# The v rows of the context's experts, one token at a time, on TensorE's column groups

## The chip, the cores and the metric
One core of one Trainium2 chip runs the whole program. The metric is the device time of one execution in microseconds. All data is f32.

## The reference
Two blocks of two layers each, on 256 tokens of width 1024. The first block is dense, the second has a feed-forward of experts (PEER): every token picks 8 x 16 of 16384 experts, and each expert is one row of a table `u` and one row of a table `v`.

```python
def first_block(x, ...):
    for l in range(2):
        h = rmsnorm(x, norm_mix[l])
        ... = split(h @ w_in[l])
        mix = concatenate([mlstm(...), moba(...), nsa(...)])
        x = x + mix @ w_out[l]
        u = square(relu(rmsnorm(x, norm_ffn[l]) @ w_ff1[l]))
        x = x + u @ w_ff2[l]
    return x

def peer_block(hb, w_q, sub_keys, u_tab, v_tab):
    ...
    expert = take_along_axis(cand_i, pos, axis=-1)
    g = softmax(top_s)
    u = u_tab[expert]
    act = gelu(einsum('nhkd,nd->nhk', u, hb))
    w = g * act
    return einsum('nhk,nhkd->nd', w, v_tab[expert])

def second_block(x, c, ctx, c_ctx, ...):
    xc = ctx
    for i in range(2):
        h, hc = modulate(rms_norm(x)), modulate(rms_norm(xc))
        x = x + g1 * (attention(q, concatenate([kc, k]), concatenate([vc, v])) @ w_o[i])
        if i == 0:
            xc = xc + cg1 * (context_attention(qc, kc, vc) @ w_o[i])
        x = x + g2 * peer_ffn(modulate(rms_norm(x)), ...)
        if i == 0:
            xc = xc + cg2 * peer_ffn(modulate(rms_norm(xc)), ...)
    return x
```

The change is about the last line, the experts of the 256 context tokens in layer 0 of the second block. They depend on nothing of the first block.

## The kernel before
**Stages.** The program has six in a row: `attention(part="context")` from 0 to some 323 us; `first_blocks`, layer 0 to 849 us and layer 1 from 885 to 1404; `attention(part="latents")` to 1708; `experts` of the latents; `attention(part="last")`; `experts` of the last layer to the end. Each engine has its own function in a stage (`sync`, `scalar`, `vector`, `gpsimd`, `tensor`), and runs it in the order in which it is written, with semaphore waits between the engines. There is no planner: the order is written by hand.

**PSUM.** `Stage` (L101) deals out the eight banks as four pairs in rotation, by a list of groups. `freed(g)` is the wait of PE for a pair, `empties(g)` its release.

**The experts of the context** are the class `Beside` (L1195), done beside `first_blocks` and the latents' attention. 256 tokens are two tiles of 128 partitions, and a tile has 128 rows of each table: row n is, for each of the 128 tokens, its n-th expert. So one row is one gather of 128 x 1024 f32, 0.52 MB, an indirect DMA that POOL issues (L1266). There are four slots for u rows and four for v rows. A step s of `vector` (L1219) is a dot of u row s with the normed tokens (L1237), and an accumulation of v row s - 16 times its weight into the context's residual `xc` (L1256). After every eight dots come some small operations of DVE (L1227 to L1246) and one power on POOL (L1278) for the gelu. `gpsimd` (L1268) issues the gathers and waits until the step that used a slot before is done.

**Where the steps stand.** `beside.vector(e, n)` is written into the vector function of each stage: 47 steps in layer 0's mixing, of them 25 in its attention part, 56 in its feed-forward, 101 in layer 1 in the same places, the remaining 68 through the latents' attention (`more(n)`, L480). `mark` notes how many steps are placed where DVE hands POOL a variance, so that POOL's gathers up to there stand ahead of its power (L1930, L744).

**A layer of the first block** (`tensor`, L1945): the turned activations hT; the projections (q and k, gates, o and v as L174 matmuls); M, the mLSTM's gates spread by a selector (L1993); the remaining projections `nat` 1 and 2; the head turns QT; the compression cmp; scores, softmax and outputs of six pairs of heads, in ping-pong with DVE and ACT (the attention part); the turn of the mix (mixT); `wo`; ff1 in eight chunks, ff2 in eight chunks (L2159). At the end of layer 0's ff2 DVE does the routing of heads 4 to 7 of the second tile of context tokens (`routed`, L1897), through ACT's exponentials `head_exp` (L1600).

**The latents' attention** (`attention`, L181): hT, three projections of q, k and v, then DVE norms and rotates queries and keys (L602) ahead of five turns QT, then 16 heads, a softmax each.

**The modulation** (L763) is in the context stage: weights of 128 x 2, 512 columns, outputs at partitions 0, 32, 64 and 96.

## Time and profile before

| what | value |
|---|---|
| median of 3 runs | 3325.4 us (3320.01 to 3327.51) |
| span of the profiled execution | 3318.4 us |
| PE busy | 2516.6 us, 76% |
| DVE busy | 2160.5 us, 65% |
| POOL busy | 1324.5 us, 40% |
| ACT busy | 475.9 us, 14% |
| moved by DMA | 1046.73 MB, mean 315 GB/s |
| of it by the gathers' queue (q0) | 805.37 MB |

The span is the time from the first to the last instruction of one execution; the runs are timed separately and contain a little more. Busy times are sums over the whole program and say which engine has work, not which one is waited for.

### The profile page before, as it was taken

The numbers are of one execution on the slowest core, as the hardware profiler recorded it, in microseconds if no ns is written. First come the engines' busy times: TensorE is split into PE (matmuls) and PEld (weight loads), VectorE is DVE, ScalarE is ACT, GpSimd is POOL, SyncE is SP. The second block draws the span as 40 slices with busy tenths as digits, with TensorE's granted clock in tenths as the row PEclk, the third lists the DMA queues.
The fourth block names the chain that finished last, engine by engine and source line by source line (L and its number), as shares of the span: only waits on it lengthen the run. The fifth ranks groups of instructions, "written<-read, shape, count | busy, mean of one in ns | idle before, by whom it ended". The sixth has DMA issues, their size and how long they took to land. (4 is left out here: it accounts for less than half of the span.)

```text
span 3318.4 us, 25154 instructions
## 1 busy us (share of the span) xinstructions
PE 2516.6 (76%) x7884; PEld 1405.9 (42%) x7884; DVE 2160.5 (65%) x5153; ACT 475.9 (14%) x1396; POOL 1324.5 (40%) x1096
## 2 busy tenths in 40 slices
PE   6785883899586599951667888887767688888877
PEld 2354553684344376421443334343334434434332
DVE  1438458678777856648867776777436577767774
ACT  1210111000111100000111111111112111111111
POOL 0000216444553755535735444454300144444542
PEclk9998885999787699975788999999978889899998
DMA  6656748889785899996849999999751399999996
GB/s 261 256 216 232 262 148 270 304 333 351 270 337 190 276 335 384 347 338 226 283 161 419 418 418 418 422 421 421 324 188 51 117 419 419 419 419 421 421 421 280
DMA packets 249209, 1046.73 MB, mean 315 GB/s; under 512 B 20550, under 2 KB 53430, under 8 KB 176884
## 3 DMA queue, kind: packets, MB, share of 16 engines
q0 software_dynamic: 147456, 805.37, 61.5%
q1 hardware_dynamic: 93456, 222.23, 18.1%
q10 hardware_dynamic: 8164, 17.53, 1.5%
q8 instruction: 63, 1.03, 0.1%
q14 instruction: 70, 0.57, 0.1%
HBM read 1041.28 MB, written 3.77 MB: 315 GB/s over the span
## 5 line engine op out<-in xcount | busy, mean ns | idle before, releaser
L1266 POOL DMA_INDIRECT sb_beside_slots<-in_peer_uv,sb_beside_chosen x512 | 596.2, 1164 | 433.5 <-DVE sb_xc L1256 284.6
L1237 DVE SCALAR_TENSOR_TENSOR sb_beside_slots<-sb_beside_slots,sb_beside_H 128x1024 f32<-128x1024 f32 x256 | 313.1, 1224 | 221.9 <-DMA sb_beside_slots<-in_peer_uv,sb_beside_chosen 214.9
L1256 DVE SCALAR_TENSOR_TENSOR sb_xc<-sb_beside_slots,sb_beside_small,sb_xc 128x1024 f32<-128x1024 f32 x254 | 325.8, 1283 | 4.6 <-DMA sb_beside_slots<-in_peer_uv,sb_beside_chosen 1.8
L174 PE MATMUL psum<-sb_f_arena,sb_f_ring 128*128 128x256 f32 (+1 forms) x1344 | 295.9, 383 | 7.9 <-issue 7.9
L174 PEld LDWEIGHTS psum<-sb_f_arena,sb_f_ring 128*128 128x128 f32 (+1 forms) x1344 | 251.5, 188 | 51.8 <-issue 9.9
L174 PE MATMUL psum<-sb_f_ring,sb_f_arena 128*128 128x512 f32 (+2 forms) x448 | 196.5, 601 | 5.7 <-DVE sb_f_arena L1877 5.7
L1170 PE MATMUL psum<-sb_latents_ring,sb_latents_scores 128*128 128x512 f32 x304 | 149.1, 643 | 52.3 <-ACT sb_latents_scores L1128 52.3
L1170 PE MATMUL psum<-sb_last_ring,sb_last_scores 128*128 128x512 f32 x276 | 141.7, 665 | 52.9 <-ACT sb_last_scores L1128 37.9
L1170 PE MATMUL psum<-sb_beside_slots,sb_latents_scores 128*128 128x512 f32 x288 | 139.8, 631 | 34.6 <-ACT sb_latents_scores L1128 34.6
L2159 PE MATMUL psum<-sb_f_ring,sb_f_arena 128*128 128x512 f32 x384 | 165.4, 592 | 0.0
L1026 POOL DMA_INDIRECT sb_latents_ring<-in_peer_uv,sb_latents_scores x76 | 92.7, 1220 | 130.6 <-PE psum L1170 92.5
L174 PEld LDWEIGHTS psum<-sb_f_ring,sb_f_arena 128*128 128x128 f32 x448 | 87.7, 197 | 109.9 <-issue 103.6
L1026 POOL DMA_INDIRECT sb_last_ring<-in_peer_uv,sb_last_scores x69 | 78.7, 1141 | 137.3 <-PE psum L1170 99.2
L1060 DVE SCALAR_TENSOR_TENSOR sb_latents_ring<-sb_latents_ring,sb_latents_H 128x1024 f32<-128x1024 f32 x76 | 92.0, 1223 | 49.4 <-DMA sb_latents_ring<-in_peer_uv,sb_latents_scores 49.4
L1026 POOL DMA_INDIRECT sb_beside_slots<-in_peer_uv,sb_latents_scores x72 | 86.8, 1205 | 88.3 <-PE psum L1170 80.0
L1060 DVE SCALAR_TENSOR_TENSOR sb_beside_slots<-sb_beside_slots,sb_latents_H 128x1024 f32<-128x1024 f32 x72 | 87.5, 1223 | 48.2 <-DMA sb_beside_slots<-in_peer_uv,sb_latents_scores 48.2
L1170 PEld LDWEIGHTS psum<-sb_latents_ring,sb_latents_scores 128*128 128x128 f32 x304 | 61.4, 207 | 133.7 <-issue 71.8
L1060 DVE SCALAR_TENSOR_TENSOR sb_last_ring<-sb_last_ring,sb_last_H 128x1024 f32<-128x1024 f32 x69 | 83.6, 1223 | 47.3 <-DMA sb_last_ring<-in_peer_uv,sb_last_scores 47.3
L1170 PEld LDWEIGHTS psum<-sb_last_ring,sb_last_scores 128*128 128x128 f32 x276 | 57.6, 213 | 130.4 <-issue 84.1
L2159 PEld LDWEIGHTS psum<-sb_f_ring,sb_f_arena 128*128 128x128 f32 x384 | 72.9, 190 | 91.4 <-issue 91.4
L1170 PEld LDWEIGHTS psum<-sb_beside_slots,sb_latents_scores 128*128 128x128 f32 x288 | 56.4, 200 | 110.9 <-issue 65.5
L744 POOL TENSOR_TENSOR sb_last_small<-sb_last_small,sb_consts 128x8 f32<-128x8 f32 (+2 forms) x6 | 7.9, 1324 | 225.0 <-DVE sb_last_small L164 154.1
(543 smaller groups left out, 4771.9 us busy)
## 6 DMA issues: line engine op xcount, KB each, us to landing
sb_f_ring<-in_w_ff SPq DMA_DIRECT2D x32, 2048.0 KB
sb_context_ring<-in_ada_w SPq DMA_DIRECT2D x23, 2048.0 KB, 10.7
sb_f_ring<-in_w_in SPq DMA_DIRECT2D x8, 2048.0 KB
sb_f_ring<-in_w_in SPq DMA_DIRECT2D x6, 1904.0 KB
sb_context_ring<-in_peer_w_q SPq DMA_DIRECT2D x8, 1024.0 KB, 10.0
sb_beside_slots<-in_peer_uv,sb_beside_chosen POOLq DMA_INDIRECT x512
sb_f_ring<-in_w_out SPq DMA_DIRECT2D x4, 2048.0 KB
sb_latents_ring<-in_peer_w_q SPq DMA_DIRECT2D x8, 1024.0 KB, 18.2
```

Source lines behind the costliest of these rows:

```text
L174: last = e.matmul(out, a, b, start=(i == 0), stop=(i == len(terms) - 1))
L744: e.tensor_tensor(r[:, 0:n], r[:, 0:n], C("m05")[:, 0:n], ALU.pow).then_inc(rstd, 1)
L1026: e.indirect_dma_start(out=slots[n % ns], out_offset=None, in_=table, in_offset=bass.IndirectOffsetOnAxis(ap=rt["idx"][:, q % 4, k:k + 1], ...
L1060: e.scalar_tensor_tensor(out=u_of(n), in0=u_of(n), scalar=1.0, in1=H[:, turns[n // TOPK][0], :], op0=ALU.mult, op1=ALU.mult, accum_out=rt[ ...
L1170: done = e.matmul(st.pair(("acc", g))[:, half, :], diag[:, n % (4 * BATCH), :], v_of(n)[:, half * 512:(half + 1) * 512], start=(f == 0 and ...
L1237: e.scalar_tensor_tensor(out=self.u_slot[s % 4], in0=self.u_slot[s % 4], scalar=1.0, in1=self.H[:, s // (PH * TOPK), :], op0=ALU.mult, op1 ...
L1256: e.scalar_tensor_tensor(out=acc, in0=row, scalar=wn, in1=acc, op0=ALU.mult, op1=ALU.add).then_inc(self.added, 1)
L1266: return e.indirect_dma_start(out=to, out_offset=None, in_=self.table, in_offset=bass.IndirectOffsetOnAxis(ap=at, axis=0), element_offset= ...
L2159: done = e.matmul(acc[t][:, half, :], u_part[c][:, f * S + t * P:f * S + (t + 1) * P], w[:, f, half * 512:(half + 1) * 512], start=False, ...
```

## The change
The u dots stay as they are on DVE. The v rows change their shape: one gather now fetches the 128 experts of *one token* onto 128 partitions, and PE sums them over the partitions with the token's 128 weights as the stationary operand.

- The indices and the weights of a tile are turned by PE (`turn_idx`, `turn_weights`), after a cast on DVE, and kept in SBUF (`keep_idx`, `keep_weights`). The gelu of a tile is done once for all 128 rows: `low` and `weigh` on DVE, a tanh on ACT. POOL's powers for it are gone.
- `columns` is a field of 4 x 16 weight matrices of 128 x 32, zero but for one column each. It lies in the space of `xc`. POOL clears it and copies 64 tokens' weights to its diagonal, twice a tile (`set_columns`).
- Four tokens are a group: 8 matmuls (L1339) with 32 weight columns and 512 moving columns, for tokens 32 partitions apart, into the last pair of PSUM. A tile has 32 groups that accumulate there. So the stages `first_blocks` and latents have three pairs for everything else. ACT copies the sums out (`tile_summed`, `all_summed`), and the latents' experts wait for it (`summed`, 3).
- One ring of eight slots serves u and v rows. The order is u rows 0 to 143, v rows of tile 0, u rows 144 to 255, v rows of tile 1.
- Where they stand: 65 dots in layer 0's mixing (25 in its attention part), 79 in its feed-forward, none in layer 1's mixing, 100 in its feed-forward (10 to each chunk of ff1, 20 after), 12 at the start of the latents' attention. The 32 groups of tile 0 stand in layer 1's mixing on PE: 2 ahead of hT, 6 after v, 4 ahead of `nat` 1, 4 after `nat` 2, 4 after the first two QT, 4 after the first turned softmax, 4 after the turned compressed keys, 4 after the fifth scores. Those of tile 1 in the latents' attention: 2 after hT, 2 after each projection and 4 more, 1 after each of five QT, 1 after each of 15 heads.
- `block.tensor` is written ahead of `block.gpsimd` in `Stage.run`, since POOL's marks now need PE's places too.

```diff
@@ class Stage
-    def __init__(self, nc, sems, psum, order, after=None):
+    def __init__(self, nc, sems, psum, order, after=None, pairs=4):
@@ class Beside
-    LAG, DEEP = 16, 4
-    STEPS = 2 * PH * TOPK + 16
+    SLOTS, GROUPS, AHEAD = 8, 32, 8
+    STEPS = NT * PH * TOPK
+    EARLY = 144
...
+    def tensor(self, e, groups):
+        upto = min(self.at_tensor + groups, NT * self.GROUPS)
+        for n in range(self.at_tensor, upto):
+            t, i = divmod(n, self.GROUPS)
+            if i % 16 == 0:
+                e.wait_ge(self.columns_set, n // 16 + 1)
+            rows = [self.landed_row(e, ("v", 4 * n + j)) for j in range(4)]
+            for half in range(2):
+                for j in range(4):
+                    done = e.matmul(self.sums[32 * j:32 * j + 32, half, :], self.columns[:, j, i % 16, :], rows[j][:, half * 512:(half + 1) * 512], start=(i == 0), stop=(i == self.GROUPS - 1))
+            done.then_inc(self.added, 1)
+        self.at_tensor = upto
...
+    def set_columns(self, e, a):
+        t, half = divmod(a, 2)
...
+        e.wait_ge(self.wT_ready, t + 1)
+        if a == 0:
+            e.memset(self.columns[:, :, :, :], 0.0).then_inc(self.cleared, 1)
...
+        e.tensor_copy(diagonal(half), weights).then_inc(self.columns_set, 1)
+
+    def gather(self, e, i):
+        kind, n = self.rows[i]
+        if i >= self.SLOTS:
+            was, m = self.rows[i - self.SLOTS]
+            e.wait_ge(*((self.dotted, m + 1) if was == "u" else (self.added, m // 4 + 1)))
...
@@ first_block, tensor
+        rows(2)
...
             natural(name, weights_of(name), 0, MW)
+        rows(6)
         sel = C("sel").rearrange("p (h m) -> p h m", h=4)
         ps = claim("M")
...
+        rows(4)
         e.wait_ge(*landed(("nat", 1)))
         natural(("nat", 1), weights_of(("nat", 1)), 0, 476)
+        mark(1)
...
         natural(("nat", 2), weights_of(("nat", 2)), 0, 476)
+        rows(4)
...
         heads_turned(1)
+        rows(4)
...
         p_turned(0)
+        rows(4)
@@ attention, tensor
-        for c, g in qkv:
+        rows(2)
+        for n, (c, g) in enumerate(qkv):
             e.wait_ge(*landed(wqkv_of[c]))
             project(("qkv", c, g), weights_of(wqkv_of[c]), (g, g + 1))
+            mark(n + 1)
+            rows(2)
+        rows(4)
@@ first_block, vector
-            beside.vector(e, 2 if routes else 4)
+            beside.vector(e, 10 if last else 6 if routes else 8)
```

PE where layer 1 begins, from ff2 of layer 0 to the remaining projections. Before (L168 is the turn hT, L174 the projections, L1993 is M):

```order
L168 MATMUL psum<-sb_consts,sb_f_hn 128x128 x16
L174 MATMUL psum<-sb_f_arena,sb_f_ring 128x256 x64
L174 MATMUL psum<-sb_f_arena,sb_f_ring 4x256 x16
L174 MATMUL psum<-sb_f_ring,sb_f_arena 128x468 x16
L174 MATMUL psum<-sb_f_ring,sb_f_arena 128x512 x32
L1993 MATMUL psum<-sb_f_hn,sb_consts 128x256 x4
L168 MATMUL psum<-sb_consts,sb_f_hn 128x4 x4
L174 MATMUL psum<-sb_f_ring,sb_f_arena 128x476 x16
L2008 MATMUL psum<-sb_f_attn 128x256 x4
L2012 MATMUL psum<-sb_f_attn 128x128 x4
```

Now (L1339 are the groups, eight matmuls each; L2132 is M):

```order
L1339 MATMUL psum<-sb_beside_slots,sb_xc 32x512 x16
L168 MATMUL psum<-sb_consts,sb_f_hn 128x128 x16
L174 MATMUL psum<-sb_f_arena,sb_f_ring 128x256 x64
L174 MATMUL psum<-sb_f_arena,sb_f_ring 4x256 x16
L174 MATMUL psum<-sb_f_ring,sb_f_arena 128x468 x16
L174 MATMUL psum<-sb_f_ring,sb_f_arena 128x512 x32
L1339 MATMUL psum<-sb_beside_slots,sb_xc 32x512 x48
L2132 MATMUL psum<-sb_f_hn,sb_consts 128x256 x4
L168 MATMUL psum<-sb_consts,sb_f_hn 128x4 x4
L1339 MATMUL psum<-sb_beside_slots,sb_xc 32x512 x32
L174 MATMUL psum<-sb_f_ring,sb_f_arena 128x476 x16
L2149 MATMUL psum<-sb_f_attn 128x256 x4
```

Two groups stand ahead of the turn hT, six between the projections and M, four between the gates' turn and the next projection.

PE in layer 1's attention part now, from the turn of the first softmax (L2191 are scores, L2231 is the compressed keys' projection):

```order
L168 MATMUL psum<-sb_consts,sb_f_attn 128x128 x4
L1339 MATMUL psum<-sb_beside_slots,sb_xc 32x512 x32
L168 MATMUL psum<-sb_consts,sb_f_arena 128x128 x12
L2231 MATMUL psum<-sb_f_cw,sb_f_small 15x64 x2
L168 MATMUL psum<-sb_consts,sb_f_attn 128x128 x8
L174 MATMUL psum<-sb_f_N,sb_f_attn 128x64 x4
L2191 MATMUL psum<-sb_f_arena 128x128 x4
L174 MATMUL psum<-sb_f_N,sb_f_attn 128x64 x8
L2191 MATMUL psum<-sb_f_arena 128x256 x4
L168 MATMUL psum<-sb_consts,sb_f_kv 128x15
L1339 MATMUL psum<-sb_beside_slots,sb_xc 32x512 x32
L168 MATMUL psum<-sb_consts,sb_f_attn 128x128 x4
```

Four groups stand behind the first turned softmax, and four more behind the turned compressed keys (`sb_f_kv`); before, these places had nothing between their neighbours.

POOL from the last rows of layer 0 to the first of layer 1. Before (L1924 and L1926 are the norm of layer 1's input, L1278 the gelu's power):

```order
L1266 DMA sb_beside_slots<-in_peer_uv,sb_beside_chosen 128x1024 x7
L1924 TENSOR_SCALAR sb_f_small<-sb_f_small 128x1
L1926 TENSOR_TENSOR sb_f_small<-sb_f_small,sb_consts 128x1
L1924 TENSOR_SCALAR sb_f_small<-sb_f_small 128x1
L1926 TENSOR_TENSOR sb_f_small<-sb_f_small,sb_consts 128x1
L1266 DMA sb_beside_slots<-in_peer_uv,sb_beside_chosen 128x1024 x9
L1278 TENSOR_TENSOR sb_beside_small<-sb_consts,sb_beside_small 128x8
L1266 DMA sb_beside_slots<-in_peer_uv,sb_beside_chosen 128x1024 x16
L1278 TENSOR_TENSOR sb_beside_small<-sb_consts,sb_beside_small 128x8
```

Now (L2053 and L2055 are that norm, L2059 the powers of the mixing; `sb_beside_small` holds the turned indices, so its gathers are v rows):

```order
L1382 DMA sb_beside_slots<-in_peer_uv,sb_beside_chosen 128x1024 x71
L1382 DMA sb_beside_slots<-in_peer_uv,sb_beside_small 128x1024 x4
L2053 TENSOR_SCALAR sb_f_small<-sb_f_small 128x1
L2055 TENSOR_TENSOR sb_f_small<-sb_f_small,sb_consts 128x1
L2053 TENSOR_SCALAR sb_f_small<-sb_f_small 128x1
L2055 TENSOR_TENSOR sb_f_small<-sb_f_small,sb_consts 128x1
L1382 DMA sb_beside_slots<-in_peer_uv,sb_beside_small 128x1024 x4
L1358 MEMSET sb_xc 128x2048
L1364 COPY sb_xc<-sb_beside_chosen 128x4x16
L1382 DMA sb_beside_slots<-in_peer_uv,sb_beside_small 128x1024 x48
L2059 TENSOR_TENSOR sb_f_small<-sb_f_small,sb_consts 128x2x8
L1382 DMA sb_beside_slots<-in_peer_uv,sb_beside_small 128x1024 x16
```

The last u rows and the first four v rows stand ahead of the norm; behind it come four v rows, then the columns' clearing and copy, then 48 v rows (12 groups) ahead of the first power of the mixing.

## Rows read from the trace of the kernel before

**Rows 1.** page, part 1 and the slices: busy us of PE, and GB/s
```profile
PE 2516.6 (76%) x7884; PEld 1405.9 (42%) x7884; DVE 2160.5 (65%) x5153; ACT 475.9 (14%) x1396; POOL 1324.5 (40%) x1096
...
GB/s 261 256 216 232 262 148 270 304 333 351 270 337 190 276 335 384 347 338 226 283 161 419 418 418 418 422 421 421 324 188 51 117 419 419 419 419 421 421 421 280
```

**Rows 2.** busy time by stretch: PE, PEld, DVE, ACT, POOL, clock, DMA share, GB/s
```profile
440.00:584.00 144.00, 75.86 (x381) 63.06 (x379) 113.50 (x230) 23.68 (x69) 75.27 (x58) 0.64 0.66 223
892.00:1000.00 108.00, 97.78 (x311) 57.97 (x310) 77.27 (x138) 15.00 (x26) 58.52 (x47) 0.91 0.84 315
1000.00:1139.00 139.00, 73.08 (x366) 60.82 (x365) 113.00 (x230) 22.72 (x68) 74.28 (x58) 0.63 0.68 230
1180.00:1292.00 112.00, 111.72 (x515) 97.96 (x516) 74.78 (x113) 8.11 (x8) 64.20 (x54) 1.00 0.98 372
1500.00:1560.00 60.00, 8.52 (x28) 6.38 (x28) 48.00 (x83) 2.99 (x5) 35.35 (x26) 0.50 0.60 202
```

**Rows 3.** page, part 5: the groups of the rows beside
```profile
L1266 POOL DMA_INDIRECT sb_beside_slots<-in_peer_uv,sb_beside_chosen x512 | 596.2, 1164 | 433.5 <-DVE sb_xc L1256 284.6
L1237 DVE SCALAR_TENSOR_TENSOR sb_beside_slots<-sb_beside_slots,sb_beside_H 128x1024 f32<-128x1024 f32 x256 | 313.1, 1224 | 221.9 <-DMA sb_beside_slots<-in_peer_uv,sb_beside_chosen 214.9
L1256 DVE SCALAR_TENSOR_TENSOR sb_xc<-sb_beside_slots,sb_beside_small,sb_xc 128x1024 f32<-128x1024 f32 x254 | 325.8, 1283 | 4.6 <-DMA sb_beside_slots<-in_peer_uv,sb_beside_chosen 1.8
```

**Rows 4.** groups by line, DVE, from 466 to 584 (layer 0's attention part)
```profile
L1256 DVE SCALAR_TENSOR_TENSOR sb_xc<-sb_beside_slots,sb_beside_small,sb_xc 128x1024 f32<-128x1024 f32 x24 | 30.7, 1281 | 0.1
L1237 DVE SCALAR_TENSOR_TENSOR sb_beside_slots<-sb_beside_slots,sb_beside_H 128x1024 f32<-128x1024 f32 x25 | 30.4, 1218 | 11.4 <-DMA sb_beside_slots<-in_peer_uv,sb_beside_chosen 11.3
```

**Rows 5.** groups by line, DVE, from 1446 to 1708 (latents' front)
```profile
L1256 DVE SCALAR_TENSOR_TENSOR sb_xc<-sb_beside_slots,sb_beside_small,sb_xc 128x1024 f32<-128x1024 f32 x63 | 80.7, 1281 | 3.3 <-DMA sb_beside_slots<-in_peer_uv,sb_beside_chosen 1.8 <-DMA sb_latents_mod<-kept_mod 0.5
L1237 DVE SCALAR_TENSOR_TENSOR sb_beside_slots<-sb_beside_slots,sb_beside_H 128x1024 f32<-128x1024 f32 x49 | 59.9, 1221 | 43.1 <-DMA sb_beside_slots<-in_peer_uv,sb_beside_chosen 42.9
```

**Rows 6.** waits of PE, 330 to 1720: total, times, longest
```profile
PE psum L168 <- DVE sb_latents_scores L602: 60.3, 3, 32.0
...
PE psum L168 <- DVE sb_f_small L1854: 21.3, 2, 10.6
PE psum L174 <- DVE sb_f_kv L1812: 18.9, 2, 9.4
```

**Rows 7.** timeline of PE, layer 1's mixing: start, us, idle before
```profile
884.84 3.91 PE L168 MATMUL psum<-sb_consts,sb_f_hn 128*128 128x128 f32 x16 [35.81 <-ACT sb_f_hn L1502]
...
978.22 3.75 PE L1993 MATMUL psum<-sb_f_hn,sb_consts 4*128 4x256 f32 x8 [10.22 <-DVE sb_f_hn L1655]
...
1000.37 12.94 PE L174 MATMUL psum<-sb_f_ring,sb_f_arena 128*128 128x476 f32 x32
...
1132.66 3.67 PE L168 MATMUL psum<-sb_consts,sb_f_hn 128*128 128x128 f32 x16 [14.85 <-DVE sb_f_hn L1792]
1139.49 30.24 PE L174 MATMUL psum<-sb_f_ring,sb_f_arena 128*128 128x512 f32 x64 [3.16 <-DVE sb_f_arena L1877]
```

**Rows 8.** timeline of PE: two bursts of the modulation, one of ff2
```profile
103.40 3.51 PE L763 MATMUL psum<-sb_context_ring,sb_cvec 128*2 128x512 f32 x16 [4.51 <-DMA sb_context_ring<-in_ada_w]
108.37 1.90 PE L763 MATMUL psum<-sb_context_ring,sb_cvec 128*2 128x512 f32 x16 [1.46 <-DMA sb_context_ring<-in_ada_w]
...
738.12 41.36 PE L2159 MATMUL psum<-sb_f_ring,sb_f_arena 128*128 128x512 f32 x96
```

**Rows 9.** timeline of POOL and DVE from 490 to 496: gathers, and a dot
```profile
490.92 1.01 POOL L1266 DMA_INDIRECT sb_beside_slots<-in_peer_uv,sb_beside_chosen  x1 [0.19 <-issue]
...
492.24 0.94 POOL L1266 DMA_INDIRECT sb_beside_slots<-in_peer_uv,sb_beside_chosen  x1 [0.30 <-issue]
...
495.38 1.23 DVE L1237 SCALAR_TENSOR_TENSOR sb_beside_slots<-sb_beside_slots,sb_beside_H 128x1024 f32<-128x1024 f32 x1 [0.96 <-DMA sb_beside_slots<-in_peer_uv,sb_beside_chosen]
```

**Rows 10.** weight loads: modulation (20 to 120), and projections (page, part 5)
```profile
L763 PEld LDWEIGHTS psum<-sb_context_ring,sb_cvec 128*2 128x2 f32 x128 | 3.1, 95 | 35.6 <-DMA sb_context_ring<-in_ada_w 22.4 <-issue 13.3
...
L174 PEld LDWEIGHTS psum<-sb_f_arena,sb_f_ring 128*128 128x128 f32 (+1 forms) x1344 | 251.5, 188 | 51.8 <-issue 9.9
```

More of the change, by code:

```diff
@@ L482, in more @@
                 beside.vector(e, steps)
+        n_marks = [0]
         def mark():
             if beside:
-                beside.mark((part, sum(1 for m in beside.marks if m[0] == part)))
+                beside.mark_vector((part, n_marks[0]))
+                n_marks[0] += 1
+        more(Beside.STEPS)
+        if beside:
+            beside.low(e, 1)
         e.wait_ge(*st.computed("cT"))
@@ L741, in gpsimd @@
             if beside:
-                beside.gpsimd(e, beside.marks[part, turn] + 1)
+                beside.gpsimd(e, beside.marks[part, turn])
             e.wait_ge(var, turn + 1)
@@ L812, in tail_group, with rows, mark @@
                 transposes(group, rows2)
+        def rows(n):
+            if beside:
+                beside.tensor(e, n)
+        def mark(turn):
+            if beside:
+                beside.mark_tensor((part, turn))
+        if beside:
+            beside.turn_weights(e, 1)
+        mark(0)
         if context:
@@ new lines, in gpsimd @@
+    def gpsimd(self, e, done):
+        dots, weights, groups = done
+        over = next((i for i, (kind, n) in enumerate(self.rows) if n >= (dots if kind == "u" else 4 * groups)), len(self.rows))
+        while self.at_gpsimd < len(self.actions):
+            what, i = self.actions[self.at_gpsimd]
+            if i >= over + self.AHEAD if what == "gather" else (i // 2 >= weights or 16 * i > groups):
+                break
+            (self.gather if what == "gather" else self.set_columns)(e, i)
+            self.at_gpsimd += 1
@@ L1621, in vector, with dots @@
         own = Tally(dve)
+        def dots(n):
+            if not gone:
+                beside.vector(e, n)
         if gone:
             e.wait_ge(gone.squared, 8)
+        else:
+            beside.cast_idx(e, 0)
         e.memset(QKp[:, :, 0:3], 0.0).then_inc(*own.up())
@@ L1634, in vector @@
                     e.scalar_tensor_tensor(out=qk[:, b, :], in0=QKp[:, b, j:j + S], scalar=cols[:, b, j:j + 1], in1=qk[:, b, :], op0=ALU.mult, op1=ALU.add).then_inc(*own.up())
-            beside.vector(e, 3)
+            dots(4)
+            if not gone and i == 0:
+                beside.keep_idx(e, 0)
         e.wait_ge(*own.now)
@@ L1828, in vector @@
         heads_out(1)
-        beside.vector(e, 2)
+        dots(2)
         scores(3)
@@ L1842, in vector @@
         dens(2)
-        beside.vector(e, 2)
+        dots(2)
         scores(4)
-        beside.vector(e, 1)
+        dots(1)
         e.wait_ge(p_exp, 1)
@@ L1855, in vector @@
         dens(3)
-        beside.vector(e, 2)
+        dots(2)
         e.wait_ge(*st.computed("cy"))
@@ L2120, in tensor @@
         scores(5)
+        rows(Beside.GROUPS - beside.at_tensor if gone else 0)
         p_turned(4)
@@ L2146, in tensor @@
             done.then_inc(st.mm, 1)
+            if last and c == 3:
+                beside.turn_idx(e, 1)
         acc = [claim(name) for name in accs]
@@ L2156, in tensor @@
                 blocks[l + 1].column_group(e)
+            if c == 6 and not last:
+                beside.turn_weights(e, 0)
             for f, t in [(f, t) for f in range(4) for t in range(NT)] if c < 7 else [(f, t) for t in range(NT) for f in range(4)]:
```

311 lines of the change are left out of this document (187 added, 124 removed).

## Prediction

> **What bounds the kernel now.** I read the page first. The line of PE shows 2516.6 us of 3318.4 busy, and the line of GB/s shows a plateau of 418 to 422 GB/s in the slices of both expert stages [rows 1]. Those stages wait for memory and the change does not touch them, so I leave them at their time. What it touches are the 256 u rows and 256 v rows that are handled beside the first block and the latents' attention.
>
> Next the busy time by stretch [rows 2]. The first block alternates. In the projections (892 to 1000) and in ff1 (1180 to 1292) PE is busy 91 to 100% of the time and DVE has room. In the attention parts (440 to 584 and 1000 to 1139) DVE is busy 113.5 of 144 us and 113.0 of 139 us, PE only about half. In the latents' query and key norms (1500 to 1560) DVE has 48.0 of 60 us and PE 8.5. So DVE bounds the attention parts and the norms, PE the rest.
>
> Who fills DVE there: the page's groups [rows 3]. The v accumulation takes 254 x 1.283 = 326 us, the u dot 256 x 1.224 = 313 us, and the dot waits 214.9 us for its gathers. In layer 0's attention part 24 accumulations are 30.7 us and gather waits 11.3 us [rows 4]; from 1446 to 1708 they are 80.7 and 42.9 us [rows 5].
>
> Last, what PE waits for. Three waits for the norms, 60.3 us in all; two for the compressed keys, 18.9 us; two for the selection, 21.3 us [rows 6]. The timeline of layer 1 adds 35.81 us at the boundary of the layers, 10.22 ahead of M, 14.85 ahead of mixT [rows 7].
>
> **Price of the parts.** *Removed:* 326 us of DVE, with the small operations per eight rows. *Moved:* in layer 1's mixing DVE now has no such work at all; its 100 dots follow in ff1 and ff2. *Added:* 64 groups of 8 matmuls on PE, each for four tokens.
>
> A group on PE: the modulation already sends 8 matmuls of 512 columns to outputs 32 partitions apart. Such a burst took 3.51 us at 103.40 and 1.90 us at 108.37 (16 records, two for each matmul); the full-width ff2 shows 96 records, 48 matmuls, in 41.36 us, 0.86 each [rows 8]. The groups follow waits, so both speeds will occur: I take the middle, 2.7 us (bounds 1.9 and 3.5).
>
> The rows of a group: gathers leave POOL 1.24 us apart (492.24 after 490.92, then 0.94 busy and 0.30 idle for each), and the one issued at 490.92 is used at 495.38, 4.5 us later [rows 9]. The ring holds eight rows, two groups. A group's four slots are refilled and landed 3 x 1.24 + 4.5 = 8.2 us after the group ends. So a burst of four has its first two groups at 2.7 and 5.4 us, the third at 2.7 + 8.2 + 2.7 = 13.6, the fourth, whose gathers queue behind those of the third, at 18.6. A burst of six ends at 29.5, and one that follows another within a few us pays about 4 more, since the ring is not full yet. A steady stream has a group each (8.2 + 2.7) / 2 = 5.5 us. **That is the crux:** PE waits in the burst, and all that stands behind it on PE waits too.
>
> *Layer 0.* 24 accumulations and the 11.3 us of gather wait leave an attention part that DVE bounds: 42 us at most. With DVE relieved, PE's and ACT's own chains end some waits, so I take 32 (bounds 20 and 45, the small operations counted in the second).
>
> *Boundary.* PE waited 35.81 us, through ACT, for the last routing on DVE. That routing now comes earlier. But two groups stand ahead of hT, behind four more gathers on POOL, a clearing of the columns and their copy: 2 x 3.5 + 5.0 us, plus the norm. The gain lies between 0 and 24; I take 13.
>
> *Layer 1's mixing.* The burst of six after v: 29.5 us, of which the old 10.22 us ahead of M hides part, +19. The four after cn come 4 us behind it, 22.6. The four after nat2, 18.6. This stretch had PE 97.8 of 108 us busy, so all 60 us lie on the path. In the attention part stand four bursts, 23 + 3 x 18.6 = 79 us. PE's own work there is about 55 us (73.1 [rows 2] less the 12.9 of the last projection and the turn of the mix [rows 7]). DVE's own work shrinks to some 50 us (113.0 less the 61 of dots and accumulations that layer 0's same part shows [rows 4]) and goes on under the bursts, which cover most of the old waits (18.9 and 21.3 for two layers, 14.85); I leave 10 uncovered. That is 144 us against some 119 now, from the end of the last projection at 1013.3 to the turn of the mix at 1132.66 [rows 7]: +25. With the boundary: 60 + 25 - 13 = **+72** (bounds +40 and +95: bursts at 1.9 us and all waits covered, or at 3.5 with the chains behind one another).
>
> *Feed-forward.* The stretches are PE's. In layer 1's ff1, DVE has 10 dots per chunk, 13.1 us of 13.8. I cost it at nothing: the squares have two buffers and the ring eight rows. If gathers and weights (8 x 2 MB, and 80 rows of 0.5 MB, 140 us at 420 GB/s in a stage of 112) hold each other up, it costs up to 20.
>
> *Latents.* Two groups after hT hide in the wait for the weights. Two after each of the first two projections: 11 us. The six after the last (29.5) and five more between the head turns (5.5 each) make some 58 us and take the place of the three waits of 60.3 us: nothing gained. Of the 124 us of accumulations and gather waits that leave DVE from 1446 to 1708, 60 lie in those waits; of the other 64, beside the heads, PE pays one group per head, so I credit 24. Sum **-13** (bounds -35 and +10).
>
> *PSUM.* Three pairs in place of four: no wait of PE in these rows names a pair, I take 0 (up to +10).
>
> Sum: -32 + 72 - 13 = **+27 us** on the profiled 3318.4. The median of the runs is 7 us above that span, so the forecast is 3325.4 + 27 = **3352 us**.
>
> **A rule weighed.** In the modulation the weight loads of 128x2 take 95 ns each, a load of 128x128 takes 188 [rows 10], and 8 matmuls with their loads still fit in 1.90 us: there the loads cost nothing visible. The new weights are 128x32, between the two. The Trainium skill (TensorE: Matmul & The Clock Gate, part 3 on packing small matmuls) says that a weight load overlaps a matmul in flight only where the row group differs, which column groups never do. By that rule the loads would be exposed. It gets a rival of its own.
>
> **Rivals.**
> 1. *The relief is worth more than the bursts* (faster). Place: layer 0's attention part and the latents' front. If PE follows DVE there one for one, they give 45 and 35 us, and with layer 1 at +55 the sum is -25: 3300 us. It decides for faster once the two give over what layer 1 loses. For it: 214.9 us of gather waits and 326 us of DVE. Against it: in the latents PE itself now waits for the same queue of gathers.
> 2. *Near cancellation*: layer 1 at +45, because bursts fall into waits that were there anyway. 3325 us.
> 3. *Exposed weight loads* (the rule). 16 load records a group at 95 to 188 ns are 1.5 to 3.0 us more for each; half of it falls into gather waits. 64 x 2.2 / 2 = 70 us: 3420 us. The bursts of rows 8 speak against it.
> 4. *The change does not do what it says*: column groups with 32 weight columns do not run at once. Then a group is 8 x 0.86 = 6.9 us, 4.2 more, 64 groups 134 to 268 us: some 3550 us. The same rows speak against it.
>
> **Chances.** A measurement of this kernel can tell about 0.2%, 6.6 us, from no change. My own case, slower by some 10 to 80 us: 0.56. Rival 1: 0.27. Rival 2: 0.10. Rival 3: 0.04. Rival 4: 0.03. So faster 0.27, same 0.10, slower 0.63. The bounds of the terms add up to 3283 at one end (-45 + 40 - 35) and about 3410 at the other (-20 + 95 + 10). Not all ends meet; the range is 3285 to 3395, which holds rivals 1 and 2 and leaves out 3 and 4. My own case alone is 3335 to 3400.
>
> **What would show it.** Right: in layer 1's mixing the matmuls of the groups wait for gathers, 6 to 8 us at a time from the third of each burst on, over 80 us in all, and from hT to wo some 340 us pass where 255 did. In layer 0 the same stretch is about 30 us shorter, and the gap ahead of hT about 20 us. A group takes 1.9 to 3.5 us. Wrong: waits for gathers under 40 us in layer 1, or a latents' front that ends 30 us nearer to its start (then rival 1), or groups of 5 us and more (3 or 4), or gaps in ff1, or PE waiting for a PSUM pair.

## The result

The changed kernel takes 3377.99 us in the median of four runs (3373.37 to 3384.34), the kernel before 3323.36 beside it: a ratio of 1.0165, 95% interval 1.0148 to 1.0183: 1.7% slower. That is +55 us where +27 was forecast.

Its page. The first lines are the engines' busy time and the throughput by slice, the others the groups of the rows beside:

```profile
PE 2655.6 (79%) x8912; PEld 1416.6 (42%) x8912; DVE 1817.4 (54%) x4657; ACT 479.6 (14%) x1401; POOL 1277.1 (38%) x1072
...
GB/s 256 252 230 231 302 194 238 332 362 243 157 261 261 282 180 404 409 288 318 313 125 346 419 419 418 419 422 421 397 162 75 60 419 419 419 419 421 421 422 282
...
L1382 POOL DMA_INDIRECT sb_beside_slots<-in_peer_uv,sb_beside_chosen x256 | 355.7, 1390 | 391.0 <-DVE sb_beside_slots L1282 205.0
L1282 DVE SCALAR_TENSOR_TENSOR sb_beside_slots<-sb_beside_slots,sb_beside_H 128x1024 f32<-128x1024 f32 x256 | 304.7, 1222 | 118.6 <-DMA sb_beside_slots<-in_peer_uv,sb_beside_chosen 89.0
L1382 POOL DMA_INDIRECT sb_beside_slots<-in_peer_uv,sb_beside_small x256 | 246.6, 963 | 275.5 <-PE psum L1339 203.6
L1339 PE MATMUL psum<-sb_beside_slots,sb_xc 128*32 128x512 f32 x1024 | 178.5, 833 | 163.4 <-DMA sb_beside_slots<-in_peer_uv,sb_beside_small 148.3
```

Against [rows 1] and [rows 3]: DVE's 326 us of accumulations are gone and its dots wait 89.0 us for gathers where they waited 214.9. PE has 178.5 us of new matmuls (L1339; 1024 records, two for each of 512), and **163.4 us of idle time just ahead of them**, 148.3 us of it waits for gathers. The plateau of 419 to 422 GB/s of the expert stages stands as it was.

Measured at the same instructions of PE in both traces (start of hT of each layer, of `wo`, the end of ff2, the first matmul of the latents' experts), the 53.7 us between the two spans come out as

| stretch | before | after | change | forecast |
|---|---|---|---|---|
| start to hT of layer 0 | 340.3 | 347.1 | +6.7 | 0 |
| layer 0, hT to `wo` | 244.0 | 205.8 | -38.2 | -32 |
| layer 0, `wo` to end of ff2 | 264.7 | 266.3 | +1.7 | 0 |
| end of ff2 to hT of layer 1 | 35.8 | 15.3 | -20.5 | -13 |
| layer 1, hT to `wo` | 254.7 | 355.0 | **+100.3** | +85 |
| layer 1, `wo` to end of ff2 | 264.8 | 262.2 | -2.6 | 0 |
| end of ff2 to the latents' hT | 26.4 | 29.3 | +2.9 | -13, with the next |
| latents, hT to the experts | 277.8 | 281.4 | **+3.6** | |
| all after that | 1609.9 | 1609.7 | -0.2 | 0 |

The timeline of PE in layer 1's mixing (start, duration, PE, line, records, and the idle time before with what ended it) answers to [rows 7]:

```profile
834.54 1.97 PE L168 MATMUL psum<-sb_consts,sb_f_hn 128*128 128x128 f32 x16
...
916.76 3.64 PE L1339 MATMUL psum<-sb_beside_slots,sb_xc 128*32 128x512 f32 x32
929.62 3.64 PE L1339 MATMUL psum<-sb_beside_slots,sb_xc 128*32 128x512 f32 x16 [9.22 <-DMA sb_beside_slots<-in_peer_uv,sb_beside_small]
934.71 3.64 PE L1339 MATMUL psum<-sb_beside_slots,sb_xc 128*32 128x512 f32 x16 [1.45 <-DMA sb_beside_slots<-in_peer_uv,sb_beside_small]
943.61 3.64 PE L1339 MATMUL psum<-sb_beside_slots,sb_xc 128*32 128x512 f32 x16 [5.26 <-DMA sb_beside_slots<-in_peer_uv,sb_beside_small]
948.71 3.64 PE L1339 MATMUL psum<-sb_beside_slots,sb_xc 128*32 128x512 f32 x16 [1.47 <-DMA sb_beside_slots<-in_peer_uv,sb_beside_small]
952.28 2.18 PE L2132 MATMUL psum<-sb_f_hn,sb_consts 4*128 4x256 f32 x8
...
1189.53 27.70 PE L174 MATMUL psum<-sb_f_ring,sb_f_arena 128*128 128x512 f32 x64 [0.99 <-ACT sb_f_arena L1699]
```

The first row is hT of layer 1, the second the first two groups of the burst of six after v (x32, 3.64 us for both, at full speed). Then PE waits 9.22 us, does a group, waits 1.45, does the next, waits 5.26. The groups after a wait take 3.64 us each, twice as long; from 929.62 to 933.26 the granted clock was 0.50, from 916.76 to 920.40 it was 1.00. Two groups pass in 14.0 us (929.62 to 943.61). `wo` starts at 1189.53, 355 us after hT.

POOL's timeline in the same burst shows the other half of the cycle:

```profile
918.99 0.93 POOL L1382 DMA_INDIRECT sb_beside_slots<-in_peer_uv,sb_beside_small  x1 [76.94 <-PE psum L1339]
920.23 0.93 POOL L1382 DMA_INDIRECT sb_beside_slots<-in_peer_uv,sb_beside_small  x1 [0.30 <-issue]
...
933.55 0.94 POOL L1382 DMA_INDIRECT sb_beside_slots<-in_peer_uv,sb_beside_small  x1 [4.95 <-PE psum L1339]
...
937.28 0.93 POOL L1382 DMA_INDIRECT sb_beside_slots<-in_peer_uv,sb_beside_small  x1 [0.31 <-issue]
```

POOL had waited 76.94 us, through all the projections, because the ring lay full; the first group frees four slots and the gathers leave 1.24 us apart. The group that began at 929.62 ends at 933.26; its slots are asked for at 933.55, and the gather that leaves last, at 937.28, is followed by a group at 943.61. So a refill is 943.61 - 933.26 = 10.3 us.

Busy time by stretch (columns as in [rows 2]: PE, PEld, DVE, ACT, POOL, then PE's granted clock, DMA share, GB/s):

```profile
834.00:917.00 83.00, 79.45 (x284) 48.30 (x280) 18.04 (x41) 13.80 (x28) 6.23 (x7) 0.98 0.43 149
917.00:981.00 64.00, 35.03 (x174) 8.64 (x167) 1.37 (x3) 4.45 (x14) 33.95 (x37) 0.65 0.87 312
1083.00:1165.00 82.00, 46.68 (x302) 17.68 (x302) 15.91 (x39) 9.47 (x31) 44.50 (x47) 0.77 0.83 289
```

Through the projections DVE is busy 18 of 83 us, and the memory queues move 149 GB/s where [rows 2] had 315 in about the same work. Then come 64 us of bursts in which PE is busy 35, its clock granted 0.65, DVE 1.4, and the DMA engines are busy 0.87. The next row is the attention part with DVE busy 15.9 of 82 us: it is no bound there any more.

What PE waited for, from 320 to 1800 us (in all, times, longest; compare [rows 6]):

```profile
PE psum L1339 <- DMA sb_beside_slots<-in_peer_uv,sb_beside_small: 148.3, 40, 12.6
PE psum L168 <- DMA sb_f_small<-in_b_if: 40.5, 1, 40.5
PE psum L168 <- DVE sb_beside_chosen L1313: 19.7, 1, 19.7
PE psum L1339 <- POOL sb_xc L1364: 13.7, 2, 9.2
```

The three waits for the latents' norms (60.3 us), those for the selection and the compressed keys are gone from the head of the list. One row took their place.

### The profile page after: what moved, and what is told of

It reads as the page before. It is cut to its first block and busy times, and to the rows that moved or that the text cites. A ratio compares the mean times of both kernels' runs of the same rounds, so it can differ in the third digit from the quotient of the medians.

```text
span 3372.1 us, 26588 instructions
## 1 busy us (share of the span) xinstructions
PE 2655.6 (79%) x8912; PEld 1416.6 (42%) x8912; DVE 1817.4 (54%) x4657; ACT 479.6 (14%) x1401; POOL 1277.1 (38%) x1072
## 5 line engine op out<-in xcount | busy, mean ns | idle before, releaser
L1382 POOL DMA_INDIRECT sb_beside_slots<-in_peer_uv,sb_beside_chosen x256 | 355.7, 1390 | 391.0 <-DVE sb_beside_slots L1282 205.0
L1282 DVE SCALAR_TENSOR_TENSOR sb_beside_slots<-sb_beside_slots,sb_beside_H 128x1024 f32<-128x1024 f32 x256 | 304.7, 1222 | 118.6 <-DMA sb_beside_slots<-in_peer_uv,sb_beside_chosen 89.0
L1382 POOL DMA_INDIRECT sb_beside_slots<-in_peer_uv,sb_beside_small x256 | 246.6, 963 | 275.5 <-PE psum L1339 203.6
L1339 PE MATMUL psum<-sb_beside_slots,sb_xc 128*32 128x512 f32 x1024 | 178.5, 833 | 163.4 <-DMA sb_beside_slots<-in_peer_uv,sb_beside_small 148.3
L174 PE MATMUL psum<-sb_f_arena,sb_f_ring 128*128 128x256 f32 (+1 forms) x1344 | 295.7, 384 | 9.0 <-issue 9.0
L174 PEld LDWEIGHTS psum<-sb_f_arena,sb_f_ring 128*128 128x128 f32 (+1 forms) x1344 | 251.9, 188 | 51.9 <-issue 10.7
L174 PE MATMUL psum<-sb_f_ring,sb_f_arena 128*128 128x512 f32 (+2 forms) x448 | 191.6, 589 | 2.0 <-ACT sb_f_arena L1699 2.0
L1339 PEld LDWEIGHTS psum<-sb_beside_slots,sb_xc 128*32 128x32 f32 x1024 | 37.2, 133 | 274.0 <-issue 253.2
L174 PEld LDWEIGHTS psum<-sb_f_ring,sb_f_arena 128*128 128x128 f32 x448 | 86.0, 194 | 104.3 <-issue 101.7
## 6 DMA issues: line engine op xcount, KB each, us to landing
sb_context_ring<-in_ada_w SPq DMA_DIRECT2D x23, 2048.0 KB, 10.9
```

The costliest lines, as they stand in the source:

```text
L174: last = e.matmul(out, a, b, start=(i == 0), stop=(i == len(terms) - 1))
L1282: e.scalar_tensor_tensor(out=row, in0=row, scalar=1.0, in1=self.H[:, t, :], op0=ALU.mult, op1=ALU.mult, accum_out=self.dots[t][:, s:s + 1] ...
L1339: done = e.matmul(self.sums[32 * j:32 * j + 32, half, :], self.columns[:, j, i % 16, :], rows[j][:, half * 512:(half + 1) * 512], start=(i ...
L1382: e.indirect_dma_start(out=self.slots[i % self.SLOTS], out_offset=None, in_=self.table, in_offset=bass.IndirectOffsetOnAxis(ap=at, axis=0) ...
```

## Experiments

My theory after the trace: the relief of DVE is large, and the price is neither PE's work nor the bytes, but that PE stands in line for a ring of eight rows; a burst empties it and pays a refill for every two groups. Rivals: the matmuls' own time; the bytes; a small relief; a limit in bandwidth wherever the groups stand.

**The relief by itself.** The kernel before with

```diff
@@ Beside.vector
-            if n >= 0:
+            if False:
                 acc, wn, row = ...
@@ Beside.gpsimd
-            if 0 <= n < self.rows:
+            if False:
                 if n >= 4:
                     e.wait_ge(self.added, n - 3)
...
```

> The kernel before, without the gathers of the v rows and without their accumulation on DVE (the sum of the v rows is left out). It measures what taking the v rows away from DVE and from the four v slots is worth, without any price on PE. Theory (the relief is real, 38 us in layer 0's mixing and 20 at the layers' boundary as the changed kernel shows, the same again in layer 1's mixing, and some 50 in the latents' front; what ate it is the wait for gathers on PE): some 3323 - 150 = 3175 us, at most 3210. Rival (DVE's relief was small from the start): over 3260 us.

Measured 3152.19 us against 3319.06, ratio 0.9494 (0.9455 to 0.9532): 167 us less. It also takes 134 MB of gathers from the memory queues, so it holds more than DVE's relief. The rival of a small relief falls.

**PE's work by itself.** The changed kernel, v rows neither fetched nor waited for:

```diff
@@ Beside.tensor
-            rows = [self.landed_row(e, ("v", 4 * n + j)) for j in range(4)]
+            rows = [self.slots[self.place["v", 4 * n + j] % self.SLOTS] for j in range(4)]
@@ Beside.gather
...
+        if kind == "v":
+            return
```

> The changed kernel with all 512 matmuls on PE, but without the gathers of the v rows and the waits for them (PE sums what lies in the slots; v rows are left out). Theory (the cost is the wait for the refill of the ring, 148 us of waits in the trace of the changed kernel): 3378 - 148 and some 40 of other waits that come out in their place, so 3270 us, within 3240 to 3300, below the kernel before. Rival (the matmuls themselves cost it, 178 us busy at half clock in part): 3340 us or more.

Measured 3158.42 us, ratio 0.9512 (0.9484 to 0.9541), 82 us below the theory's lower end. Its rows: the group of the matmuls in the page, and the burst of six with the one of four in the timeline.

```profile
L1339 PE MATMUL psum<-sb_beside_slots,sb_xc 128*32 128x512 f32 x1024 | 121.3, 616 | 6.3 <-POOL sb_xc L1364 5.1
...
908.53 10.51 PE L1339 MATMUL psum<-sb_beside_slots,sb_xc 128*32 128x512 f32 x96
...
921.08 8.77 PE L1339 MATMUL psum<-sb_beside_slots,sb_xc 128*32 128x512 f32 x64
```

The same 512 matmuls take 121.3 us in place of 178.5, 1.9 us for each group (the burst of six 10.51 us in one piece, in place of 35.6 with its waits), and stand behind 6.3 us of idle time. The run stands within 6 us of the one without v rows at all, but that is not the price of the matmuls: the two also differ in where the dots stand and in the depth of their ring. In layer 1 from hT to `wo`, with 32 groups that are 61 us busy and no dots, it takes 231.5 us against 219.4, 12 more; in layer 0's mixing, without groups, it is 17 us *shorter*, and in the latents' front, with the other 32, 18 us. So the matmuls' own price is small beside 220 us but was not measured by itself. Against the changed kernel 220 us are missing. The page closes that account: 163.4 - 6.3 = 157 us of waits, 178.5 - 121.3 = 57 us because the groups after a wait run at the lower clock, 6 us besides. The run also spares the memory queues 134 MB.

**Half of each group's matmuls, full gathers.**

```diff
-            for half in range(2):
+            for half in range(1):
```

> The changed kernel with full gathers, but 4 of the 8 matmuls of each group (the second half of the width is left out). Theory (refill of the ring): the waits for gathers stay at 130 to 160 us, and only the matmuls' own time falls, 178 to about 90 busy, of which a part goes into longer waits: 3378 - 50 = 3330 us. Rival (the matmuls' time is the cost): 3378 - 89 = 3290 us or less, the waits no longer than now.

Measured 3346.31 us, 32 less. The waits for gathers *rose* from 148.3 to 178.5 us: what the matmuls gave back, the waits took. A group fell from 3.64 to 1.94 us, and two of them still pass in 12.5 us (932.02 to 944.49). The rival (89 us less) is out; the theory's own 50 us was too much as well. The waits rose above the 130 to 160 us that it had.

**Half of the bytes.** As that run, and each v gather fetches 512 columns.

```diff
+        if kind == "v":
+            e.indirect_dma_start(out=self.slots[i % self.SLOTS][:, 0:512], ..., element_offset=D)
...
```

> As the run with 4 of 8 matmuls, and each v gather fetches only the first 512 of 1024 columns (half the bytes, the same 128 descriptors' worth of rows and the same issue time on POOL). Theory (a fixed issue and landing time per group of four rows): the waits for gathers fall by at most a quarter against the run with full gathers, the time by 10 to 35 us. Rival (the bytes are what PE waits for): the waits halve, the time falls by 60 us or more.

Measured 3321.61 us, 25 less than with full gathers. The waits fell from 178.5 to 126.4 us, 29%, a little more than the quarter that I had allowed and far from half. In layer 1 they fell from 109.7 to 84.1, but waits for DVE, ACT and POOL (7.0, 5.9 and 5.3 us) came out in their place, and from hT to `wo` it is 342.1 us against 347.9; the rest of the gain is in the latents, where they fell from 68.8 to 42.3. So half of the bytes take 29% of the waits away: issue and landing of four rows are the larger part of the cycle, but the bytes are a part of it.

Half of the matmuls:

```profile
PE psum L1339 <- DMA sb_beside_slots<-in_peer_uv,sb_beside_small: 178.5, 41, 14.5
...
932.02 1.94 PE L1339 MATMUL psum<-sb_beside_slots,sb_xc 128*32 128x512 f32 x8 [3.17 <-DMA sb_beside_slots<-in_peer_uv,sb_beside_small]
938.80 1.94 PE L1339 MATMUL psum<-sb_beside_slots,sb_xc 128*32 128x512 f32 x8 [4.84 <-DMA sb_beside_slots<-in_peer_uv,sb_beside_small]
944.49 1.93 PE L1339 MATMUL psum<-sb_beside_slots,sb_xc 128*32 128x512 f32 x8 [3.75 <-DMA sb_beside_slots<-in_peer_uv,sb_beside_small]
```

Half of the bytes as well:

```profile
PE psum L1339 <- DMA sb_beside_slots<-in_peer_uv,sb_beside_small: 126.4, 32, 11.2
...
928.56 1.94 PE L1339 MATMUL psum<-sb_beside_slots,sb_xc 128*32 128x512 f32 x8 [1.18 <-DMA sb_beside_slots<-in_peer_uv,sb_beside_small]
935.14 1.94 PE L1339 MATMUL psum<-sb_beside_slots,sb_xc 128*32 128x512 f32 x8 [4.64 <-DMA sb_beside_slots<-in_peer_uv,sb_beside_small]
940.27 1.94 PE L1339 MATMUL psum<-sb_beside_slots,sb_xc 128*32 128x512 f32 x8 [3.19 <-DMA sb_beside_slots<-in_peer_uv,sb_beside_small]
```

Busy time in layer 1's bursts, first with all bytes, then with half:

```profile
926.92:969.18 42.26, 17.57 (x68) 4.76 (x69) 1.37 (x3) 3.56 (x13) 25.01 (x27) 0.50 0.96 345
...
925.45:962.44 36.99, 17.52 (x69) 4.75 (x70) 1.46 (x3) 3.55 (x13) 24.81 (x28) 0.50 0.65 189
```

With all bytes the DMA engines are busy 0.96 of the stretch, so there two groups could hardly pass faster than in the 12.5 us measured, whatever the depth of the ring; the changed kernel's bursts had 0.87. With half of the bytes they have room, and a pair takes 11.7 us here. In the latents it takes 12.2 us with all bytes (1569.09 to 1581.31) and 10.0 with half (1561.83 to 1571.88), where POOL issues its gathers 1.25 us apart without a pause, eight in 10.0 us. So below the ring's cycle two other limits lie close, the DMA engines and POOL's issue.

**Half of the ring.**

```diff
-    SLOTS, GROUPS, AHEAD = 8, 32, 8
+    SLOTS, GROUPS, AHEAD = 4, 32, 4
...
```

> The changed kernel with a ring of four rows in place of eight, so that one group lies in it and not two; nothing else changed. Theory (cycle of the ring: a group's four slots are refilled some 10 us after it ends, and with two groups in the ring each costs half a cycle of 13.6 us): every group now costs the whole cycle, 6.8 us more where PE waits for them, some 50 of 64 groups: 3378 + 340 = 3700 us, within 3600 to 3800, the waits for gathers over 400 us. The dots of DVE, with four slots, gain some waits too, under cover of PE. Rival (the bandwidth of the gathers or their issue on POOL sets the pace, not the depth): under 3450 us.

Measured 3819.7 us, ratio 1.1502 (1.1469 to 1.1534): 442 us more than with eight slots. That is 120 us above the theory's number and outside its range of 3600 to 3800. It shows the cycle bare:

```profile
PE psum L1339 <- DMA sb_beside_slots<-in_peer_uv,sb_beside_small: 525.6, 55, 15.1
...
1002.23 3.64 PE L1339 MATMUL psum<-sb_beside_slots,sb_xc 128*32 128x512 f32 x16 [9.78 <-DMA sb_beside_slots<-in_peer_uv,sb_beside_small]
1015.42 3.64 PE L1339 MATMUL psum<-sb_beside_slots,sb_xc 128*32 128x512 f32 x16 [9.56 <-DMA sb_beside_slots<-in_peer_uv,sb_beside_small]
...
1028.89 3.64 PE L1339 MATMUL psum<-sb_beside_slots,sb_xc 128*32 128x512 f32 x16 [7.48 <-DMA sb_beside_slots<-in_peer_uv,sb_beside_small]
1042.69 3.64 PE L1339 MATMUL psum<-sb_beside_slots,sb_xc 128*32 128x512 f32 x16 [10.16 <-DMA sb_beside_slots<-in_peer_uv,sb_beside_small]
```

Now every group behind the first of a burst waits, most of them 7.5 to 10.7 us, and takes 3.64: 13.2 to 14.3 us from start to start in the rows shown, one group in each, where the ring of eight passes two. The waits are 525.6 us. Layer 1 takes 538 us from hT to `wo` (864.8 to 1403.1), the ring of eight 355. From 975.28 to 1070.27 the DMA engines are busy 0.46, and the refill still takes some 10 us, as it does in the ring of eight at 0.87. So at four rows the depth sets the pace, and neither the bandwidth nor POOL's issue does; at eight POOL's timeline above shows the same refill, but, as the run with half of the matmuls shows, with little room left below it. Part of the excess over the theory lies where it had put nothing: layer 0's hT to layer 1's hT is 521 us in place of 487. 19 of these 34 us lie ahead of the end of ff2, where only dots of DVE use the ring; the other 15 are the two groups ahead of hT.

**The groups spread.** The same groups at other places of layer 1's mixing, nothing else moved (`i == 0` is the first of four projection pieces):

```diff
-        rows(2)
...
             done.then_inc(st.mm, 1)
+            rows(2 if i == 0 else 1)
...
+        rows(1)
         natural(("nat", 0), w, 8, 468)
+        rows(2)
         for name in ("o", "v"):
             e.wait_ge(*landed(name))
             natural(name, weights_of(name), 0, MW)
-        rows(6)
+            rows(2)
...
-        rows(4)
+        rows(1)
         e.wait_ge(*landed(("nat", 1)))
         natural(("nat", 1), weights_of(("nat", 1)), 0, 476)
         mark(1)
+        rows(2)
...
         natural(("nat", 2), weights_of(("nat", 2)), 0, 476)
-        rows(4)
+        rows(2)
...
         heads_turned(1)
-        rows(4)
```

and the other 15 in ones and twos between the scores, turns and outputs of the attention part.

> The changed kernel with only the places of the 32 groups in layer 1's mixing moved: none ahead of hT, one or two after every projection unit (at most two in a row, some 7 us of matmuls for each group), singles through the attention part. Theory (a burst drains the ring of eight rows and waits for its refill; between bursts the ring lies full): from hT to wo 260 to 285 us where the bursts took 355 and the run without v gathers 231, and the time 3378 - 85 = 3293 us, within 3275 to 3320, so faster than the kernel before. Rival (the gathers' bandwidth in that stretch is the limit, wherever the groups stand): 3350 us or more, with the same sum of waits for gathers.

Measured 3290.13 us, ratio to before 0.9914 (0.9898 to 0.9931), 88 us less than the changed kernel and within 3 us of the theory. From hT to `wo` 283.8 us (821.2 to 1105.0) where the bursts took 355.0. So the order alone turns a loss of 1.7% into a gain of 0.9%, with the same gathers, matmuls and ring. The rival, a limit of bandwidth wherever the groups stand, forecast 3350 us or more and falls. The waits for gathers are not gone, 95.1 us are left.

**Spread among the projections only**, the last 12 groups in three bursts of four:

> As the spread one in the projections and the compression, 20 groups, but the last 12 stand in three bursts of four in the attention part as in the changed kernel. Theory: each burst there costs about 23 us of PE, of which the attention part, with DVE relieved, hides little; so 20 to 45 us slower than the run with all spread, 3315 to 3335 us. Rival (only the bursts among the projections matter, where PE is the bound): within 8 us of the run with all spread.

Measured 3320.09 us, ratio to before 1.0007 (0.9995 to 1.0019), 30 us above the run with all spread and within the forecast 3315 to 3335. Of the 27 us between the two profiled spans 20 lie from hT to `wo` (304.2 us in place of 283.8), so the three bursts cost some 7 to 10 us each; the bursts of the other 20 groups had cost 58 together. The rival (only the bursts in PE's own stretch matter) falls: with DVE relieved, bursts in the attention part cost time too.

**The latents' burst spread as well:**

```diff
             mark(n + 1)
             rows(2)
-        rows(4)
...
+                if among[i][0] == "wo":
+                    rows(1)
```

> As the spread one, and in the latents' front the four extra groups after the last projection (with the two there, a burst of six, 37 us in the trace of the changed kernel) are moved: one after each of the last heads and after each wo. Theory: the burst goes down to two groups and the four others find their rows landed, 15 to 30 us less than the spread run, 3260 to 3280 us. Rival (the latents' front is bound by the gathers as a whole, 128 rows of 0.52 MB): no more than 6 us less.

Measured 3280.08 us, ratio 0.9880 (0.9862 to 0.9898), 10 us less; the theory had 15 to 30, its rival (the front is bound by the gathers as a whole) at most 6. It fits neither, and lies nearer to the rival. The timeline, in the projections of layer 1 and then in the latents:

```profile
889.60 3.64 PE L1340 MATMUL psum<-sb_beside_slots,sb_xc 128*32 128x512 f32 x32
893.17 14.00 PE L174 MATMUL psum<-sb_f_ring,sb_f_arena 128*128 128x512 f32 x32
907.11 3.64 PE L1340 MATMUL psum<-sb_beside_slots,sb_xc 128*32 128x512 f32 x32
...
1477.82 3.64 PE L1340 MATMUL psum<-sb_beside_slots,sb_xc 128*32 128x512 f32 x16 [7.89 <-DMA sb_beside_slots<-in_peer_uv,sb_beside_small]
...
1483.05 1.92 PE L1340 MATMUL psum<-sb_beside_slots,sb_xc 128*32 128x512 f32 x16 [0.54 <-DMA sb_beside_slots<-in_peer_uv,sb_beside_small]
...
1491.49 3.64 PE L1340 MATMUL psum<-sb_beside_slots,sb_xc 128*32 128x512 f32 x16 [5.92 <-DMA sb_beside_slots<-in_peer_uv,sb_beside_small]
...
1496.55 1.92 PE L1340 MATMUL psum<-sb_beside_slots,sb_xc 128*32 128x512 f32 x16 [0.37 <-DMA sb_beside_slots<-in_peer_uv,sb_beside_small]
...
1505.52 3.64 PE L1340 MATMUL psum<-sb_beside_slots,sb_xc 128*32 128x512 f32 x16 [6.46 <-DMA sb_beside_slots<-in_peer_uv,sb_beside_small]
```

Among long projections two groups a time find their rows there: 3.64 us for both, no wait. In the latents nothing long stands between the head turns, so the pattern of 13.7 to 14.0 us for two groups (1477.82 to 1491.49 to 1505.52) is there without any burst. 32 groups at half of 13.7 would be 219 us, an estimate, of the 274 that this front takes. From 1395 to 1590 the DMA engines are busy 0.92 of the time, at 329 GB/s. So up to there this front is near what its gathers allow in any order, and no run parts the share of the ring's cycle from that of the DMA engines.

**Fewer gathers ahead of layer 0.**

```diff
+        ahead = 4 if done == (0, 0, 0) else self.AHEAD
```

> The changed kernel with four gathers in place of eight issued ahead of the norm of layer 0's input, as the kernel before did. Theory (the wait of PE for the bias at the start, 40.5 us where it was 34.6, comes from four more gathers of 0.5 MB ahead of it in the memory queues): hT at about 341 us in place of 347, 3372 us in the median, 3 to 8 us less. Rival: the wait has another cause, no change.

Measured 3381.52 us, the same as the changed kernel within its runs, where 3 to 8 us less were expected. PE still waits 40.0 us for the bias, so four gathers more ahead of it are not the cause. The four held back leave at 330.3, right behind the norm. hT starts at 344.4 where it was 347.1, but in the ten traces with the new ring it starts anywhere between 343.5 and 348.8 us, and at 340.3 and 342.4 in the two with the old slots. The cause of the later start stays open.

**The best version**: all spread, and 12 dots from the latents' start into layer 1's ff2.

```diff
         if last:
-            beside.vector(e, 20)
+            beside.vector(e, 32)
```

> The run with all groups spread, and the last 12 dots of the second tile stand at the end of layer 1's ff2 (32 there in place of 20) and no longer at the start of the latents' front. Theory (PE waits 19.7 us there for the weights of the second tile, behind these dots on DVE, and DVE and the gathers have room in ff2): the wait shrinks, but hT behind it waits for the norm anyway, so 3 to 10 us less than 3280, some 3273 us. Rival (the norm sets the start): no change.

Measured 3266.34 us, ratio 0.9837 (0.9818 to 0.9855): 57 us less than the kernel before, 112 less than the changed one, 14 less than the run ahead of it (3 to 10 were expected; the two ran at different times, each beside its own runs of the kernel before, whose medians differ by 3 us). PE's wait for the weights fell from 19.7 to 7.7 us, and from the end of ff2 to the latents' hT it takes 18.7 us in place of 29.3. It still waits 88.6 us for gathers.

## Why the prediction was right, and where it was half the size

**What held.** The sign, the mechanism and its place: waits for gathers inside the bursts, over 80 us of them in layer 1 (89.4 in the trace), 355 us from hT to `wo` (some 340 forecast). They begin at the third group where long work stands ahead of the burst (929.62, 1022.00, 1099.80), and at the first or second in the others. They are not 6 to 8 us each: a wait of 3 to 12.6 us is followed in most bursts by one of 1.4 to 1.9. The relief in layer 0 (-38.2 for -32) and at the boundary (-20.5 for -13) came, both a little larger. A group takes 1.9 to 3.64 us. The dots of ff1 cost nothing; no wait of PE names a pair of PSUM.

**The step that failed** is the price of the cycle, "a group's four slots are refilled and landed 3 x 1.24 + 4.5 = 8.2 us after the group ends" and "I take the middle, 2.7 us". Both terms were small. The refill measures about 10 us (10.3 at 943.61, waits of 9.5 to 10.7 in most of layer 1 with the ring of four): I had taken the landing of the first of four gathers, the one at 490.92 [rows 9], with none issued in the 20 us before it, and the last of four lands later (937.28 to 943.61, 6.3 us from its issue). And the group behind a wait takes 3.64 us, not the middle, at a granted clock of 0.50: all ten groups behind more than 5 us of idle time took 3.4 to 3.64, and without the waits the same groups took 1.9. So two groups mostly take 13.2 to 14.6 us, not 10.9, some 6.9 for one in a steady stream and not 5.5. Bursts of four measured 22 to 29 us, the wait ahead of them counted, where I had 18.6 to 23, the ten groups after v 61 us in place of 52. That is the larger part of layer 1's +100 for +85.

**The term with the wrong sign** is the latents, -13 forecast and +6.5 measured with the gap ahead of it. Its parts, before and after: hT to the end of the last projection 59.4 and 65.0 us (+5.5, 11 forecast), from there to the end of the last turn 65.4 and 68.8 (+3.4, nothing forecast), and from there to the experts, beside the heads, 153.0 and 147.6 (-5.3, where I had credited 24). So the step that failed here is the 24 us of relief beside the heads. The run without v gathers needs 196 us for this front, the changed kernel 281: 85 us of waits and slow groups ate nearly all of what the relief gave. The price of the cycle is behind this term too: I let PE pay one group a head at 2.7 us and put no wait there, and beside the heads PE waited 17.2 us for gathers and 4.5 for the columns.

**The start**, +6.7 us, had no term. The run with four gathers fewer did not settle it.

**Luck.** Layer 1 and the latents came out 35 us above their terms, the start 7. The reliefs of layer 0 and the boundary, 6 and 8 us larger than forecast, hid part of that. The lower end of the range was also added up wrongly: -45 + 40 - 35 from 3325.4 is 3285, not 3283; nothing hangs on it.

**The rivals.** The first, that the relief beats the bursts, had a large relief right: without v rows the kernel is 167 us faster. It fell because the waits were dearer still. The exposed weight loads: 16 load records of 128x32 with a median of 111 ns, and still a group back to back takes 1.9 us, as the bursts of [rows 8] did with loads of 128x2. The rule of the Trainium skill (TensorE: Matmul & The Clock Gate, part 3) that a load overlaps a matmul only where the row group differs (it names a load into the background weight buffer as a second case) would have added, by an estimate from these records, 16 x 0.111 = 1.8 us to each group; this case's trace does not show that. Column groups do run at once with 32 weight columns: 8 matmuls of 512 columns in 1.9 us, where 8 full-width ones take 6.9.

## What to carry to other kernels

A ring of prefetched rows hides a transfer only if its consumer comes back no sooner than a refill takes; so place consumers one or two at a time between long pieces of other work, and never more in a row than the ring holds. Price a burst as its length less the depth of the ring, each further pair at a full cycle of issue, landing of the *last* transfer in the queue, and the work at the clock that a waiting engine gets. When work moves to another engine, ask what that engine's queue is then waiting for: here 167 us of relief were there, 220 us of waits and slowed matmuls stood against it, and the order of the same instructions decided the sign. And look at how busy the transfer engines are before making a ring deeper: at 0.96, as in the run with half of the matmuls, depth has little more to give.
